# Down product of two token chunks by seven products of half-size blocks instead of eight, its block sums made on VectorE and GpSimd

## The chip, the cores and the metric

The kernel runs on one core of a Trainium2 chip. The metric is device time in microseconds (us) of one execution; the profile's span runs from the first to the last instruction of one such execution.

## What is computed

The reference is one step of a two-layer encoder trunk over 1024 prompt tokens and 64 sample tokens, all in float32. Only the last part of each layer matters here, the down-projection of the feed-forward part; the rest is projection, gating, attention and a recurrent memory.

```python
D_MODEL = 1024; DEPTH = 2; SEQ = 1024; DEC_SEQ = 64; D_FF = 2816; CONV_W = 3

def conv_ffn(x, g, w_up, conv_w, conv_b, w_down, conv_buf):
    up = rmsnorm(x, g) @ w_up
    T = up.shape[1]
    full = jnp.concatenate([conv_buf.astype(up.dtype), up], axis=1)
    c = conv_b + full[:, 0:T] * conv_w[0]
    for j in range(1, CONV_W):
        c = c + full[:, j:j + T] * conv_w[j]
    y = (jax.nn.gelu(c[..., :D_FF], approximate=False) * c[..., D_FF:]) @ w_down
    return y, full[:, -(CONV_W - 1):]

def layer(x, pos, lp, cache):
    ...
    x = x + mixed @ lp['w_out']
    y, conv_state = conv_ffn(x, lp['ffn_norm'], lp['w_up'], lp['conv_w'], lp['conv_b'], lp['w_down'], conv_buf)
    x = x + y
    ...
```

## The kernel before

The program is written engine by engine, each engine's instructions in an order fixed by hand, with counting semaphores between the engines. No scheduler moves anything. All activations stand transposed: features on the 128 partitions, tokens along the free axis. The residual stream `xT` stays in SBUF. Its tokens (1024 prompt, 2 of padding, 64 sample) form three chunks, `CH`: 0 and 1 of 384 columns, 2 of 322.

**Split products.** A float32 product is made of three matmuls in a reduced format (`split3`, L321 to L325). Each operand is split into a high part (ScalarE rounds a copy) and a low part (VectorE subtracts the high part from the original), and TensorE adds high by high, high by low and low by high.

**The up stage.** For each of 22 pairs `p` of up-projection columns, TensorE makes products into PSUM, VectorE combines them (`take`, L2333), ScalarE and VectorE do the convolution (`conv_first`, `tap`), the GELU and the gate product (`gate_product`, L2375), and SyncE stores the 128x1090 result to a DRAM scratch (`store_g`). `value_end` is the second half of that chain for the pair before. GpSimd makes sums of weight blocks here (`weight_sum`, L1978).

**The down stage.** The output has 8 blocks of 128 features, one PSUM bank each. For each chunk `c` and each of the 22 blocks `f` of 128 gate rows there is one step, `i = 22 c + f`:

- SyncE loads the weight row block `w_down[f]`, 128x1024 (`load_down`, 512 KB), and the gate block of the chunk, 128x384 (`load_g`, 192 KB);
- ScalarE makes the high parts (`down_high` L1716, `gate_high` L1722), VectorE the low parts (`down_low` L2380, `gate_low` L2385). The gate parts go round in four slots, so a high part of step `i` waits until TensorE is through with step `i - 4`;
- TensorE does 8 output blocks by 3 matmuls, 24 in a step (`step`), 1056 for chunks 0 and 1 of a layer.

When a chunk ends, VectorE adds the 8 banks into `xT` (`add_down`, L2062), ScalarE squares the result and GpSimd sums the squares for the next norm (`norm_add`, L371). In the last layer chunk 2 runs in two halves of 4 output blocks (`half_step`, with L2478 and L1824 for its weights).

**Names.** In the trace the gate blocks stand as `tHf` (as loaded), `tH` (high) and `tL` (low), the weights as `raw` and `wb`, and `sqE`, `sqn` and `acc` belong to the norm. DVE is VectorE, ACT ScalarE, POOL GpSimd, SP SyncE, PE TensorE.

## Time and profile before

| | before |
|---|---|
| time, median of 3 runs | 2478.15 us (2477.4 to 2478.68) |
| span of the profiled execution | 2478.2 us |
| PE (TensorE) busy | 2446.6 us, 99% of the span |
| DVE (VectorE) busy | 1588.2 us, 64% |
| ACT (ScalarE) busy | 1096.2 us, 44% |
| POOL (GpSimd) busy | 527.5 us, 21% |
| DMA | 265.89 MB, mean 107 GB/s |

The profiled execution took, by its span, what the timed runs took. Shares of busy time are means over stages with different limits: a 44% or 21% says nothing about a single stage. Matmuls are pipelined, so the durations in their rows overlap; the distance between two starts is what one costs.

### The profile page before, as it was taken

How to read it: one execution, taken by the hardware profiler on the slowest of the kernel's cores; microseconds unless marked ns; L12 is line 12 of the kernel's file. 1: busy time of each engine (PE TensorE's matmuls, PEld its weight loads, DVE VectorE, ACT ScalarE, POOL GpSimd, SP SyncE). 2: the span in 40 equal slices, each digit the busy share in tenths (PEclk: the TensorE clock that was granted, in tenths of full speed). 3: DMA queues.
4: the chain of work that ended last, by engine and by line, in shares of the span. 5: the costliest groups of instructions: out<-in, count | busy, mean ns of one | idle time of the engine just before them, and what ended most of it. 6: DMA issues, size and time to landing. Idle time of an engine off the chain costs nothing.

```text
span 2478.2 us, 41945 instructions
## 1 busy us (share of the span) xinstructions
PE 2446.6 (99%) x16611; PEld 2381.6 (96%) x16611; DVE 1588.2 (64%) x2693; ACT 1096.2 (44%) x2067; POOL 527.5 (21%) x490
## 2 busy tenths in 40 slices
PE   9999999999999999999999999999999999999999
PEld 8999888999999999999999988889999999999999
DVE  3115688878888887465611266878888888864564
ACT  6326656534333333343433355645334333343453
POOL 0001253423222220010110112433322222200110
PEclk9999999999999999999999999999999999999999
DMA  4442322122222223554525333212222222155564
GB/s 153 132 133 92 115 84 77 54 70 65 75 79 70 79 77 110 191 175 160 190 71 155 110 97 115 82 49 71 66 75 79 70 79 77 63 167 169 176 195 146
DMA packets 238072, 265.89 MB, mean 107 GB/s; under 512 B 15639, under 2 KB 207925, under 8 KB 235701
## 3 DMA queue, kind: packets, MB, share of 16 engines
q1 hardware_dynamic: 237876, 263.22, 33.5%
q8 instruction: 132, 2.16, 0.4%
q14 instruction: 64, 0.52, 0.1%
HBM read 213.06 MB, written 50.11 MB: 106 GB/s over the span
## 4 chain that ended last, share of the span: by engine, by line
PE 87%; DVE 6%; issue 3%; ACT 2%; DMA 1%; POOL 0%; SPq 0%; DVEq 0%; POOLq 0%; ACTq 0%
PE bank L323 27%; PE bank L325 26%; PE bank L324 26%; PE bank L1119 1%; PE bank L1046 1%; DMA zb<-z_scratch 1%; PE bank L1104 1%; PE bank L1088 1%; DVE actL L2265 1%; PE bank L1129 1%; PE bank L1068 1%; DVE hc L2201 0%; PE bank L1080 0%; DMA rawB<-in_w_down 0%; PE bank L999 0%
## 5 line engine op out<-in xcount | busy, mean ns | idle before, releaser
L323 PE MATMUL bank<-actH,wb 128*128 128x384 f32 (+1 forms) x1712 | 560.4, 327 | 1.8 <-DVE xT L2062 1.8
L324 PE MATMUL bank<-actL,wb 128*128 128x384 f32 (+1 forms) x1712 | 554.8, 324 | 0.0
L325 PE MATMUL bank<-actH,wb 128*128 128x384 f32 (+1 forms) x1712 | 554.4, 324 | 0.0
L323 PE MATMUL bank<-wzH,actH 128*128 128x256 f32 (+3 forms) x1296 | 369.1, 285 | 3.2 <-DVE wzL L2019 2.1
L325 PE MATMUL bank<-wzH,actL 128*128 128x256 f32 (+3 forms) x1296 | 364.2, 281 | 0.0
L324 PE MATMUL bank<-wzL,actH 128*128 128x256 f32 (+3 forms) x1296 | 363.8, 281 | 0.0
L323 PEld LDWEIGHTS bank<-actH,wb 128*128 128x128 f32 x1712 | 322.4, 188 | 7.2 <-issue 6.2
L324 PEld LDWEIGHTS bank<-actL,wb 128*128 128x128 f32 x1712 | 323.1, 189 | 0.7
L325 PEld LDWEIGHTS bank<-actH,wb 128*128 128x128 f32 x1712 | 323.2, 189 | 0.0
L323 PEld LDWEIGHTS bank<-wzH,actH 128*128 128x128 f32 (+1 forms) x1296 | 236.3, 182 | 6.1 <-issue 4.0
L323 PE MATMUL bank<-tH,wb 128*128 128x384 f32 x704 | 237.0, 337 | 1.2 <-ACT vn L1817 1.2
L324 PE MATMUL bank<-tL,wb 128*128 128x384 f32 x704 | 236.7, 336 | 0.0
L325 PE MATMUL bank<-tH,wb 128*128 128x384 f32 x704 | 236.7, 336 | 0.0
L324 PEld LDWEIGHTS bank<-wzL,actH 128*128 128x128 f32 (+1 forms) x1296 | 236.4, 182 | 0.0
L325 PEld LDWEIGHTS bank<-wzH,actL 128*128 128x128 f32 (+1 forms) x1296 | 236.1, 182 | 0.0
L1700 ACT ACTIVATE cv<-upb,convc 128x1090 f32<-128x1090 f32 x88 | 114.4, 1300 | 240.5 <-DVE upb L2357 240.3
L2380 DVE TENSOR_TENSOR wb<-raw,wb 128x1024 fp32r<-128x1024 f32 x88 | 107.8, 1225 | 169.7 <-ACT wb L1716 169.6
L1978 POOL TENSOR_TENSOR Sf<-raw 128x512 f32<-128x512 f32 x80 | 112.0, 1401 | 391.3 <-PE bank L325 382.5
L1674 ACT ACTIVATE Sx<-Sf 128x512 fp32r<-128x512 f32 x160 | 100.5, 628 | 200.1 <-POOL Sf L1978 200.1
L2333 DVE TENSOR_TENSOR upb<-bank,upb 128x384 f32<-128x384 f32 x280 | 148.1, 553 | 60.5 <-PE bank L325 57.5
L1444 ACT ACTIVATE zst<-bank,stat 128x256 f32<-128x256 f32 (+3 forms) x162 | 75.8, 473 | 240.9 <-PE bank L325 240.6
L1716 ACT ACTIVATE wb<-raw 128x1024 fp32r<-128x1024 f32 x88 | 93.2, 1061 | 198.7 <-PE bank L325 160.7
(311 smaller groups left out, 5152.5 us busy)
## 6 DMA issues: line engine op xcount, KB each, us to landing
raw<-in_w_up SPq DMA_DIRECT2D x88, 512.0 KB, 4.4
raw<-in_w_down SPq DMA_DIRECT2D x88, 512.0 KB, 3.6
g_scratch<-cv SPq DMA_DIRECT2D x44, 545.0 KB, 3.2
rawz<-in_w_in SPq DMA_DIRECT2D x22, 1024.0 KB, 5.4
zb<-z_scratch SPq DMA_DIRECT2D x16, 1156.0 KB, 5.4
tHf<-g_scratch SPq DMA_DIRECT2D x88, 192.0 KB, 3.7
z_scratch<-zst SPq DMA_DIRECT2D x128, 128.0 KB, 1.7
raw<-in_w_out SPq DMA_DIRECT2D x128, 128.0 KB, 2.8
```

The source lines that it names most:

```text
L323: pe.matmul(out, aH, bH, start=first, stop=False)
L324: pe.matmul(out, aH, bL, start=False, stop=False)
L325: return pe.matmul(out, aL, bH, start=False, stop=last)
L1046: m = pe.matmul(bank[2 * c + p // 2][64 * v:64 * v + 64, (p % 2) * 256 + k0:(p % 2) * 256 + k1], bqT[64 * v:64 * v + 64, p, 64 * c:64 * c ...
L1068: pe.matmul(bank[6][:, 0:4 * r], ones[0:r, :], dA[0:r, 0:4 * r], start=True, stop=True).then_inc(S["A_r"], 1)
L1444: act.activation(zst[0:r, u % 3, 0:w], bank[z_bank(u)][0:r, 0:w], ACT.Gelu if u < 18 else ACT.Copy, scale=rt[0:r, t:t + 1]).then_inc(z_ev, 1)
L1674: act.activation(Sx[:, s, 0], Sf[:, s, 1], ACT.Copy).then_inc(s_h, 1)
L1700: act.activation(cv[:, :], (upb2 if h else upb1)[:, PAD:], ACT.Identity, scale=convc[:, f + 88:f + 89], bias=convc[:, f + 132:f + 133]).th ...
L1716: act.activation(h, t, ACT.Copy).then_inc(w_h, 1)
L1978: pool.tensor_tensor(Sf[:, s, 1], x, y, ALU.add if s == 0 else ALU.subtract).then_inc(s_r, 1)
L2333: dve.tensor_tensor(out, bank[b][:, 0:out.shape[1]], other, ALU.mult if i in (6, 9) else ALU.add).then_inc(take_r, 1)
L2380: dve.tensor_tensor(lo, t, h.bitcast(F32), ALU.subtract).then_inc(w_l, 1)
```

## The change

The down product of chunks 0 and 1 together is a matrix of 1024 output features by 768 tokens, with 2816 rows to sum over. It is cut into halves three ways. Call the weight blocks A11 (features 0 to 511, gate rows 0 to 1407), A12 (features 0 to 511, gate rows 1408 to 2815), A21 and A22 (the same for features 512 to 1023), and the gate blocks B11, B12 (gate rows 0 to 1407, chunk 0 and 1), B21, B22 (gate rows 1408 to 2815). Eight block products become seven, each of 4 output blocks by 11 gate-row blocks (`NJ`) by 384 tokens, 12 matmuls in a step, 77 steps (`seven`), 924 matmuls:

| product q | weights | gates | added into |
|---|---|---|---|
| 0 | A21 + A22 (GpSimd) | B11 | C21, -C22 |
| 1 | A22 | B21 - B11 (GpSimd) | C11, C21 |
| 2 | A12 - A22 (GpSimd) | B21 + B22 (GpSimd) | C11 |
| 3 | A11 + A22 (GpSimd) | B11 + B22 (VectorE) | C11, C22 |
| 4 | A12 + A11 (GpSimd) | B22 | -C11, C12 |
| 5 | A11 | B12 - B22 (GpSimd) | C12, C22 |
| 6 | A21 - A11 (GpSimd) | B11 + B12 (VectorE) | C22 |

A weight tile is now 128x512 (256 KB, `load_tile`), kept in `at0` and `at1`; some are loaded again because the sums overwrite them. Gate blocks are loaded three rows at a time (`load_gates`) into `gT`, `actG` and `actF`. Chunk 2 keeps its steps, with other buffers and waits. The core of the diff:

```diff
@@ -497,30 +543,58 @@
+        def a_sum_at(l, i):
+
+            return l * N_SUM + 4 * (NF - 2) + (0, 0, 1, 2, 3, 0, 4)[i // NJ] * NJ + i % NJ + 1
+
+        def seven_bank(q, m):
+            return bank[m if q % 2 else 4 + (m + 2) % 4]
...
@@ -772,26 +846,60 @@
+                def load_tile(n, slot, f, h):
+
+                    tile_landed(sp, l, n - 7)
+                    n += NTOK + l * N_TILES
+                    sp.dma_start(a_tile(slot), w_down[f * P:f * P + P, 512 * h:512 * h + 512]).then_inc(tile_in[n % 7], 16)
...
@@ -813,16 +921,49 @@
                     if p == NF - 2:
-                        load_down(0)
-                        load_down(1)
-                for i in range(4):
-                    load_g(i)
-                load_down(2)
-                load_down(3)
+                        sp.wait_ge(w_l, weight_at(l, NF - 1, 1))
+                        sp.wait_ge(s_r, sum_at(l, NF - 1, 3))
+                        sp.wait_ge(mm, tile_mm(l, NF - 2, N_TILE))
+                        for j in range(3):
+                            load_first(j)
+                for j in range(3, 6):
+                    load_first(j)
+                sp.wait_ge(mm, tile_mm(l, NF - 1, 3))
+                for g in range(4):
+                    load_gates(0, g)
+                sp.wait_ge(mm, tile_mm(l, NF - 1, N_TILE))
+                for j in range(6, 9):
+                    load_first(j)
                 store_g(NF - 1)
+                for j in range(9, NJ):
+                    load_first(j)
...
@@ -1285,34 +1422,53 @@
+                def seven(i):
+
+                    q, j = i // NJ, i % NJ
+                    h, lo = (t.rearrange("p k n -> p (k n)") for t in seven_hl(i))
+                    pe.wait_ge(w_l, down_at(l, i))
+                    pe.wait_ge(b_l, gate_at(l, i))
+                    for m in range(4):
...
+                        s = slice(m * P, m * P + P)
+                        x = split3(pe, seven_bank(q, m)[:, 0:384], h[:, s], lo[:, s], gH[:, i % 4], gL[:, i % 4], j == 0, j == NJ - 1)
+                        if m == 3 or j == NJ - 1:
+                            x.then_inc(mm, 1)
...
@@ -1706,19 +1861,43 @@
+                def seven_high(i):
...
+                    act.wait_ge(mm, seven_mm(l, i - 4) if i >= 4 else tile_mm(l, NF - 1, (2, 4, 5, 7)[i]))
+                    act.activation(seven_hl(i)[0], a_tile(a_slot(q, j)).rearrange("p (k n) -> p k n", n=P), ACT.Copy).then_inc(w_h, 1)
+
+                def seven_gate_high(i):
...
+                    act.wait_ge(mm, seven_mm(l, i - 4) if i >= 4 else tile_mm(l, NF - 1, 2))
+                    act.activation(gH[:, i % 4], g_place(q // 4, j) if q in (0, 4) else gR[:, i % 4], ACT.Copy).then_inc(b_h, 1)
...
@@ -1997,8 +2201,44 @@
+                def a_sum(i):
...
+                    pool.tensor_tensor(t, x, y, ALU.subtract if q in (2, 6) else ALU.add).then_inc(s_r, 1)
+
+                def g_sum(i):
...
+                    pool.wait_ge(b_l, gate_at(l, i - 4))
+                    x, y = (gT[:, j], g_place(0 if q == 1 else 1, j))
+                    pool.tensor_tensor(gR[:, i % 4], x, y, ALU.add if q == 2 else ALU.subtract).then_inc(gs_r, 1)
+
                 n = 2 * l + 2
-                for c in range(3):
+                for i in range(N_SEVEN):
+                    if i // NJ in (0, 2, 3, 4, 6):
+                        a_sum(i)
+                    if i // NJ in (1, 2, 5):
+                        g_sum(i)
+                    m = i - 5 * NJ - 5
+                    if 1 <= m < KT:
+                        norm_add(pool, n, 0, m)
+                for c in range(1, 3):
...
@@ -2374,13 +2614,43 @@
+                def seven_gate_sum(i):
+
+                    q, j = i // NJ, i % NJ
+                    gates_landed(dve, l, (8 if q == 3 else 12) + j // 3)
+                    dve.wait_ge(b_l, gate_at(l, i - 4))
+                    dve.tensor_tensor(gR[:, i % 4], g_place(0, j), g_place(1, j) if q == 3 else gT[:, j], ALU.add).then_inc(gd_r, 1)
+
+                def seven_add(q):
+
+                    dve.wait_ge(bank_free, F0 + ADDED[q])
+                    for m in range(4):
+                        dve.wait_ge(mm, seven_mm(l, q * NJ + NJ - 1, m))
+                        for sign, r, c in OUTS[q]:
+                            x, y = xT[:, 4 * r + m, 384 * c:384 * c + 384], seven_bank(q, m)[:, 0:384]
+                            dve.tensor_tensor(x, x, y, ALU.add if sign > 0 else ALU.subtract).then_inc(bank_free, 1)
...
@@ -2505,38 +2774,33 @@
+                for i in range(4, N_SEVEN):
+                    if i + 2 < N_SEVEN and (i + 2) // NJ in (3, 6):
+                        seven_gate_sum(i + 2)
+                    seven_low(i)
+                    seven_gate_low(i)
+                    if i % NJ == 3 and i > NJ:
+                        seven_add(i // NJ - 1)
```

VectorE at the end of the up stage (the last pair of layer 0), before. `upb` and `cv` are the convolution's tiles:

```order
L2385 TENSOR_TENSOR tL<-tHf,tH 128x384 x4
L2333 TENSOR_TENSOR upb<-bank,rowS 128x322
...
L2380 TENSOR_TENSOR wb<-raw,wb 128x1024
L2367 SCALAR_TENSOR_TENSOR cv<-upb,convc,cv 128x1090
L2370 SCALAR_TENSOR_TENSOR cv<-upb,convc,cv 128x1090
L2375 TENSOR_TENSOR cv<-cv,cu 128x1090
L2380 TENSOR_TENSOR wb<-raw,wb 128x1024 x2
```

The same place of the changed kernel. L2621 is `seven_low`, L2628 `seven_gate_low`:

```order
L2628 TENSOR_TENSOR tL<-actG,tH 128x384 x2
L2573 TENSOR_TENSOR upb<-bank,rowS 128x322
...
L2607 SCALAR_TENSOR_TENSOR cv<-upb,convc,cv 128x1090
L2610 SCALAR_TENSOR_TENSOR cv<-upb,convc,cv 128x1090
L2615 TENSOR_TENSOR cv<-cv,cu 128x1090
L2628 TENSOR_TENSOR tL<-actG,tH 128x384
L2621 TENSOR_TENSOR wS<-at,wS 128x512
```

Before, the low gate parts of steps 0 to 3 stood ahead of the last convolution; now those of steps 2 and 3 stand behind it.

GpSimd between the up stage and the next norm (layer 0), before:

```order
L1978 TENSOR_TENSOR Sf<-Sf,raw 128x512
L1978 TENSOR_TENSOR Sf<-raw 128x512
L1978 TENSOR_TENSOR Sf<-raw,Sf 128x512
L371 TENSOR_TENSOR acc<-acc,sqE 128x384 x9
L400 TENSOR_TENSOR stat<-stat 128x3
```

The same place of the changed kernel, cut after the first two steps of product 2 and taken up again where product 3 begins. L2217 is `a_sum`, L2230 `g_sum`, L410 `norm_add`:

```order
L2182 TENSOR_TENSOR Sf<-raw,Sf 128x512
L2217 TENSOR_TENSOR at<-at 128x512 x11
L2230 TENSOR_TENSOR tHf<-gT,actG 128x384 x6
L2230 TENSOR_TENSOR tHf<-gT,actF 128x384 x5
L2217 TENSOR_TENSOR at<-at 128x512
L2230 TENSOR_TENSOR tHf<-gT,actG 128x384
L2217 TENSOR_TENSOR at<-at 128x512
...
L2217 TENSOR_TENSOR at<-at 128x512 x22
L2230 TENSOR_TENSOR tHf<-gT,actG 128x384 x6
L2230 TENSOR_TENSOR tHf<-gT,actF 128x384
L410 TENSOR_TENSOR acc<-acc,sqn 128x384
```

Where GpSimd had only the norm's sums there are now 55 weight sums and 33 gate sums in a layer, in the order of the steps.

## Rows read from the trace of the kernel before

**Rows 1.** The page: the span.

```profile
span 2478.2 us, 41945 instructions
```

**Rows 2.** Windows: A:B length, busy of PE, PEld, DVE, ACT, POOL; PEclk, DMA share, GB/s.

```profile
370.00:400.00 30.00, 29.50 (x216) 26.29 (x215) 24.62 (x62) 17.11 (x53) 11.30 (x14) 1.00 0.19 63
973.00:1158.50 185.50, 184.90 (x1060) 184.53 (x1059) 96.78 (x119) 75.41 (x107) 8.59 (x7) 1.00 0.55 179
2194.00:2379.00 185.00, 184.40 (x1057) 184.03 (x1056) 91.27 (x111) 74.65 (x109) 8.58 (x7) 1.00 0.55 179
```

**Rows 3.** Timeline of PE: start, duration; steps 0 and 44 begin the first and last.

```profile
973.00 0.34 PE L323 MATMUL bank<-tH,wb 128*128 128x384 f32 x1
...
1119.38 0.33 PE L324 MATMUL bank<-tL,wb 128*128 128x384 f32 x1
...
1129.51 0.34 PE L325 MATMUL bank<-tH,wb 128*128 128x384 f32 x1
...
1158.51 0.31 PE L323 MATMUL bank<-tH,wS 128*128 128x322 f32 x1
```

**Rows 4.** Groups by line and shape: count, busy us, mean ns, idle before.

```profile
L1978 POOL TENSOR_TENSOR Sf<-raw,Sf 128x512 f32<-128x512 f32 x40 | 52.4, 1310 | 164.6 <-PE bank L325 164.6
L2385 DVE TENSOR_TENSOR tL<-tHf,tH 128x384 fp32r<-128x384 f32 x88 | 59.9, 683 | 1.4 <-ACT tH L1722 1.4
L2062 DVE TENSOR_TENSOR xT<-bank,xT 128x384 f32<-128x384 f32 x64 | 33.5, 553 | 16.0 <-PE bank L325 15.9
L1824 ACT ACTIVATE wb<-raw 128x512 fp32r<-128x512 f32 x44 | 26.5, 624 | 14.0 <-DMA raw<-in_w_down 8.6 <-PE bank L325 5.0
```

**Rows 5.** Timelines of DVE and of POOL near 915 us (up stage).

```profile
915.43 1.22 DVE L2254 TENSOR_TENSOR wb<-raw,wb 128x1024 fp32r<-128x1024 f32 x1
916.57 2.67 DVE L2333 TENSOR_TENSOR upb<-bank,upb 128x384 f32<-128x384 f32 x5
...
915.77 2.03 POOL L1978 TENSOR_TENSOR Sf<-Sf,raw 128x512 f32<-128x512 f32 x1 [2.75 <-PE bank L325]
```

**Rows 6.** Timelines of DVE and of POOL near 2390 us (last chunk).

```profile
2389.07 1.20 DVE L2478 TENSOR_TENSOR wb<-raw,wb 128x512 fp32r<-128x512 f32 x1 [0.18 <-ACT wb L1824]
2390.20 1.31 DVE L2483 TENSOR_TENSOR actL<-tHf,actH 128x322 fp32r<-128x322 f32 x1
2391.43 0.55 DVE L2062 TENSOR_TENSOR xT<-bank,xT 128x384 f32<-128x384 f32 x1
...
2388.71 1.02 POOL L371 TENSOR_TENSOR acc<-acc,sqE 128x384 f32<-128x384 f32 x1
2389.89 1.27 POOL L371 TENSOR_TENSOR acc<-acc,sqE 128x384 f32<-128x384 f32 x1 [0.17 <-ACT sqE L362]
```

**Rows 7.** Timeline of DVE, two low parts in a row with POOL idle.

```profile
2397.27 0.68 DVE L2478 TENSOR_TENSOR wb<-raw,wb 128x512 fp32r<-128x512 f32 x1
2397.87 0.48 DVE L2483 TENSOR_TENSOR actL<-tHf,actH 128x322 fp32r<-128x322 f32 x1
2398.28 0.68 DVE L2478 TENSOR_TENSOR wb<-raw,wb 128x512 fp32r<-128x512 f32 x1
```

**Rows 8.** Timelines of DVE, ACT and SPq where the up stage of layer 0 ends.

```profile
973.27 0.49 DVE L2333 TENSOR_TENSOR upb<-bank,rowS 128x322 f32<-128x322 f32 x1 [0.20 <-PE bank L325]
979.17 1.30 DVE L2375 TENSOR_TENSOR cv<-cv,cu 128x1090 f32<-128x1090 f32 x1
...
963.07 0.53 ACT L1722 ACTIVATE tH<-tHf 128x384 fp32r<-128x384 f32 x1 [6.34 <-DMA tHf<-g_scratch]
974.12 1.04 ACT L1716 ACTIVATE wb<-raw 128x1024 fp32r<-128x1024 f32 x1
...
959.68 1.78 SPq L794 DMA_DIRECT2D tHf<-g_scratch  x4
```

**Rows 9.** DMA issues of the page and of 940 to 990 us: count, KB each, us to landing.

```profile
raw<-in_w_down SPq DMA_DIRECT2D x44, 256.0 KB, 3.1
...
GB/s 0 0 0 0 0 0 138 393 308 0 13 0 0 0 0 202 281 194 243 381 344 256 13 0 0 0 0 0 0 0 0 13 0 391 154 295 291 390 79 115
```

More of the change, by code:

```diff
@@ new lines, in _ @@
+                for j in range(NJ):
+                    load_a11(j)
+                for g in range(4):
+                    sp.wait_ge(gs_r, g_sum_at(l, 2 * NJ + min(3 * g + 3, NJ) - 1))
+                    load_gates(3, g)
+                for j in range(NJ):
+                    load_a12_again(j)
+                for j in range(9):
+                    load_a21_again(j)
+                def load_half(j):
+                    h, f = j // NF, j % NF
+                    if j < 4:
+                        sp.wait_ge(mm, tile_mm(l, NF - 1, N_TILE))
+                    else:
+                        sp.wait_ge(w_l, down_at(l, LAST0 + j - 4))
@@ L1804, in _ @@
                     else:
-                        for i in range(4):
-                            gate_high(i)
+                        seven_gate_high(0)
+                        seven_gate_high(1)
                     conv_first(p, 0)
@@ new lines, in square_second @@
+                def square_second(m):
+                    norm_square(act, n, 1, m, F0 + (ADDED[5] + 2 * m + 1 if m < 4 else ADDED[6] + m - 3))
+                if l + 1 == DEPTH:
+                    for j in range(2 * NF):
+                        half_high(j)
+                        if j < NF:
+                            gate_high_last(j)
+                        m = j - 3
+                        if 0 <= m < KT:
+                            square_second(m)
+                            act.activation(xT[:, m, 384:768], xT[:, m, 384:768], ACT.Copy,
```

539 lines of the change are left out of this document (328 added, 211 removed).

## The prediction, made before the changed kernel ran

> **What bounds the kernel now.** I read the page first: the span is 2478.2 us [rows 1]. The windows of the two stretches in which chunks 0 and 1 of a layer run say what sets the pace there: PE is busy 184.90 of 185.50 us at a granted clock of 1.00, DVE 96.78, ACT 75.41, POOL 8.59 [rows 2]. So TensorE is the bound, the others keep ahead of it, and GpSimd is nearly unused. The timeline of PE gives the price of a matmul by its starts: 59 of them from 1119.38 to 1129.51, 58 distances, 0.1747 us each; and the 1056 matmuls of chunks 0 and 1 take from 973.00 to 1158.51, 185.5 us [rows 3]. Layer 1 has the same stretch.
>
> **What TensorE gains.** 77 steps of 12 matmuls are 924 in place of 1056. At 0.1747 us that is 161.4 us, 24.1 less per layer, 48 us in the two. A step is now 12 x 0.1747 = 2.10 us, half of before, and in each step ScalarE and VectorE must still deliver one weight part and one gate part. Were TensorE still the bound, the time would be 2430 us. ScalarE is no danger: 0.62 for a 128x512 copy [rows 4] and, by the first gate copy, 0.53 [rows 8], 1.2 of 2.10 us.
>
> **What the sums cost.** The trace shows that an operation of GpSimd and one of VectorE that reads two SBUF tensors do not run at the same time. Near 2390 us [rows 6]: GpSimd works to 2389.73 (2388.71 + 1.02); VectorE's low part of a weight, issued at 2389.07, ends at 2390.27, 0.54 after it; GpSimd's next, issued at 2389.89, ends at 2391.16, 0.89 after VectorE's; VectorE's next low part ends at 2391.51, 0.35 after that. They take turns, even when VectorE's second one was already queued. Near 915 us [rows 5] it is GpSimd that waits: VectorE ends at 916.65, GpSimd at 917.80, 1.15 after, for a 128x512 sum that takes 1.31 undisturbed [rows 4]. VectorE's operations with one operand in PSUM are not in this: five ran in 2.67 us under that sum [rows 5], and one at 2391.43 in 0.55 [rows 6]. The Trainium skill says the same (SBUF — State Buffer, section Who interferes with whom): the second to issue blocks fully, if VectorE has two SBUF inputs; by that rule, the trace agrees, with 0.54, 0.89 and 0.35 us behind the other's end.
>
> So there is a shared resource, call it the port, and I add up how long it is held in one layer's chunks 0 and 1. GpSimd: 55 weight sums of 128x512 at 1.15, 63.3 us; 33 gate sums of 128x384 at 0.89, 29.4; 7 norm sums at 0.89, 6.2 (they are moved in here from chunk 1, where the port was free). VectorE: 77 low parts of 128x512 at 0.54 and 77 of 128x384 at 0.42 (0.35 x 384/322), 73.9; 22 gate sums at 0.42, 9.2. Together 182 us, in a stretch where TensorE needs 161.4. The 48 additions from PSUM (before 16) cost VectorE 12 x 4 x 0.48 = 23 us, but no port. The port, not VectorE (about 120 us) or GpSimd (about 110), is what becomes scarce.
>
> How a step goes then: with a low part pair (0.96) and nothing else 0.96; each GpSimd operation that lies between adds its hold. Product 1 (one gate sum): 1.85 us in a step, under 2.10. Product 2 (weight and gate sum): 0.96 + 1.15 + 0.89 = 3.0. Product 3 and 6 (weight sum, VectorE's gate sum): 2.53. Products 0 and 4: 2.11. The lead that may cover the excess is short: a high part of step i waits for TensorE's step i - 4, so VectorE is 3 steps ahead at most, and a gate sum of GpSimd waits for the low part of step i - 4, so GpSimd is 4 steps ahead of VectorE.
>
> **The walk through one layer**, TensorE's delay product by product:
>
> - Start of product 0. VectorE's take of the last pair starts when TensorE is through (973.27), then comes the last convolution, whose gate product ended at 980.47 [rows 8]. In the new order the low gate part of step 2 stands behind that. A 1.04 us high part [rows 8] ahead of that convolution becomes 0.62 [rows 4], so step 2 can begin at about 980.1 + 0.5 = 980.6, where TensorE wants it at 973.0 + 2 x 2.10 = 977.2: 3.4 us. Further, the first gate blocks (issued at 959.68 before, used at 963.07 [rows 8]) now queue behind the store of 545 KB and six tiles of 256 KB, 2.1 MB, which at the 250 to 390 GB/s of the bursts [rows 9] are 6 to 8 us; they arrive near 967.5, and VectorE has two low gate parts and the last pair's takes behind them. Three weight sums of GpSimd fall in the same stretch. That moves the chain by 2 to 3 us more. I take 6 us, between 3.4 and 9.
> - Products 0 and 1 are then paced by TensorE. From VectorE's step 18 GpSimd is already at product 2, so its last four steps go at 3.0: 1.2 us late.
> - Product 2. VectorE delivers step 25 about 9 us after the product begins, then adds product 1 (8 additions, 3.8 us), during which GpSimd comes to its 4-step limit. Steps 26 to 28 take 3.0 each. Then GpSimd, through with the product, runs ahead into the 11 weight sums of product 3, which wait for nothing of VectorE's; turn by turn each of VectorE's operations meets one: steps 29 and 30 cost 0.96 + 2 x 1.15 = 3.26, steps 31 and 32, with the gate sums for 33 and 34, 1.38 + 3 x 1.15 = 4.8. Sum from the start: 9 + 3.8 + 1 + 6 + 6.5 + 9.6 = 36, and the last step's own 2.1: 38 us in place of 23.1, 15.0 late.
> - Product 3 finds its sums made: 0. Product 4: the additions of product 3 use up the lead, 1.2.
> - Products 5 and 6. From step 61 to 65 gate and norm sums come in turns (2.7 a step), then GpSimd runs ahead into 11 weight sums and two norm sums while VectorE does 62 to 66 at 3.3 to 4.8 each; then product 5's additions. Product 5 takes 30.3, product 6 28.3, together 12.5 late.
>
> Sum of the delays: 6 + 1.2 + 15.0 + 0 + 1.2 + 12.5 = 36 us. A layer's stretch: 161.4 + 36 = 197.4 against 185.5, +11.9; two layers +23.8. 2478.2 + 23.8 = 2502 us; the timed median is the span's to 0.1. Moving the tail changes nothing: chunk 2 steps are long (24 matmuls) or as before. DMA traffic falls (66 tiles of 256 KB for 44 loads of 512), and 179 GB/s at a share of 0.55 [rows 2] left room; a 256 KB load lands in 3.1 us [rows 9], so the tiles, asked for some 9 steps ahead, are hidden; uncovered they would cost 3 us each. The clock: a 30 us window with DMA waits kept 1.00 [rows 2], so I count no loss.
>
> **Bounds.** If turns packed without any idle port time, the stretch is 182 less what is done before TensorE arrives (6 weight sums and the first low parts, 9 us), 173, perhaps 178 with the start: 2478 - 2 x 7.5 = 2463 us. If each operation costs its undisturbed distance (GpSimd 1.31 [rows 4] and 1.02 [rows 6], VectorE 0.60 between starts [rows 7] and 0.47), the port sum is 206, 24 more per layer, some 12 of it in the crowded products, and the start 9 instead of 6: 2502 + 2 x 13 = 2528. I take the turn-taking prices, since those rows are the same operations under the same pressure. Another price: the Trainium skill (GPSIMD Engine Reference, section Instruction dispatch) gives a two-input GpSimd body a floor of about 2.5 cycles per element. An estimate from that page, at its 1.2 GHz, is 1.07 us for 128x512 and 0.80 for 128x384; by it the sum for the port would be 174 instead of 182 and the time about 2490. The rows show 1.15 and 0.89.
>
> **Rivals.**
> - *TensorE stays the bound* (6 in 100): the short rings absorb the turns and only the start is late. For it: VectorE was busy half of the stretch and GpSimd hardly [rows 2]. Against: 182 us held in 161. It gives 2478 - 2 x (24.1 - 6) = 2442, faster.
> - *The port packs well* (18 in 100): products 2, 5 and 6 are crowded, but 0, 1 and 4 take the overflow, as GpSimd works ahead. This is the rival on the other side. It decides where the delays of a layer fall under 24.1 us instead of 36, that is, where each of the 95 GpSimd operations holds VectorE up 0.13 us less than counted. Against: VectorE's 4-slot limit forbids work ahead. It gives 2455 to 2485, centre 2468; 11 of the 18 faster, 4 within 0.2%, 3 slower.
> - *The start and the queue are worse* (10 in 100): the gate blocks land several us later, or the port's undisturbed prices hold; 2520 to 2540.
> - The forecast, the port as the bound with short leads, has 66 in 100: 2485 to 2520, 2502 the likeliest.
>
> **Numbers.** No change that can be told is within 0.2%, 5 us. Faster 0.17 (6 + 11), same 0.05 (4 and the low edge of the forecast), slower 0.78. The range runs from 2460, which leaves out the first rival and the lowest part of the second, to 2528, which leaves out most of the third: about 2 in 10 outside.
>
> **What would show it.** 924 matmuls in each layer's stretch, still 0.175 us apart when fed, clock 1.00; idle PE ahead of the high-by-high matmul put down to VectorE's low parts, some 30 us a layer, most of it in the third, sixth and seventh product; VectorE's low parts of 128x512 with a mean near 1.2 us instead of the 0.68 of [rows 7], and in the first and fifth product near 0.7; GpSimd's weight sums taking 1.7 to 1.9; step 2 of the first product beginning 3 to 9 us late. I am wrong if low parts stay at 0.7 and 0.55 us beside a busy GpSimd, if the waits are for DMA or for ScalarE, or if the delays of a layer are under 24 us.

## The result and the profile after

The changed kernel takes 2532.5 us (2529.8 to 2539.5, 4 runs), the one before 2477.8 us (2476.5 to 2478.7, 4 runs, same chip): a ratio of 1.0226, 95% interval 1.0211 to 1.0241, 55 us slower. The forecast was slower, 2502 us, with a range to 2528: the sign is right, the time lies 4.5 us above the range and 30 above the forecast. The profiled execution is the slowest of the four, 5 us above their median, so the profile's sums are a little larger than the timed difference. From here on products are counted first to seventh, as they run; the first is q = 0 of the table (the recorded expectations use both counts: "gate sums of products 1, 2 and 5" goes by q, "product 5 from 29.8" is the fifth).

The page of the changed kernel answers to [rows 1]:

```profile
span 2537.7 us, 42355 instructions
...
PE 2440.6 (96%) x16347; PEld 2360.6 (93%) x16347; DVE 1783.3 (70%) x2933; ACT 1129.0 (44%) x2199; POOL 783.8 (31%) x666
...
PE   9999999999999998898999999999999999988798
...
DVE  3115687888888887989611267877888888789874
...
POOL 0001244432222223864000113442322222358610
```

In the 16th to 19th and the 36th to 39th slice (of 63.4 us), where chunks 0 and 1 are, VectorE stands at 8 and 9, GpSimd at up to 8, and TensorE has holes. The windows of the stretch in layer 0, cut where the seven products begin (by the starts of every 132nd matmul), answer to [rows 2]; behind the length stand busy time of PE, PEld, DVE, ACT and POOL, then the granted clock:

```profile
971.40:1008.50 37.10, 29.37 (x137) 28.20 (x136) 28.98 (x38) 15.67 (x27) 12.05 (x11) 0.82 0.78 270
1008.50:1033.30 24.80, 23.72 (x134) 23.05 (x132) 24.46 (x29) 11.85 (x23) 17.91 (x14) 1.00 0.07 26
1033.30:1071.20 37.90, 28.68 (x132) 26.46 (x133) 37.90 (x36) 11.49 (x22) 33.56 (x23) 0.86 0.26 82
1071.20:1095.20 24.00, 23.59 (x134) 23.30 (x133) 23.72 (x33) 11.75 (x22) 16.66 (x8) 1.00 0.61 212
1095.20:1125.00 29.80, 25.54 (x133) 24.57 (x133) 23.57 (x34) 11.50 (x22) 15.28 (x12) 0.94 0.38 124
1125.00:1157.50 32.50, 27.30 (x134) 25.07 (x132) 31.81 (x31) 16.01 (x31) 27.44 (x20) 0.89 0.02 3
1157.50:1186.70 29.20, 25.36 (x132) 24.82 (x133) 27.07 (x43) 11.44 (x20) 5.61 (x4) 0.94 0.22 69
```

A product of 132 matmuls at 0.1747 us takes 23.06 us; the stretch is 215.3 us instead of 185.5. In layer 1 it is 214.9. The account closes: 2478.2 + 29.8 + 29.4, less 3.4 us by which the two up stages end earlier, plus 3.7 us in the tail, is 2537.7. In the third and the sixth product VectorE is busy 37.90 of 37.90 and 31.81 of 32.50 us: it is the engine that does not get through. What keeps it so long is in the groups by line and shape, which answer to [rows 4] (mean ns of one stands behind the busy time):

```profile
L2217 POOL TENSOR_TENSOR at<-at 128x512 f32<-128x512 f32 x110 | 184.1, 1691 | 91.3 <-DMA at<-in_w_down 91.0
L2621 DVE TENSOR_TENSOR wS<-at,wS 128x512 fp32r<-128x512 f32 x154 | 167.6, 1091 | 30.4 <-ACT wS L1874 30.4
L2628 DVE TENSOR_TENSOR tL<-tHf,tH 128x384 fp32r<-128x384 f32 x110 | 105.3, 957 | 0.0
L2645 DVE TENSOR_TENSOR xT<-xT,bank 128x384 f32<-128x384 f32 x96 | 46.0, 542 | 2.7 <-PE bank L361 2.7
```

Undisturbed, the low parts (L2621 and L2628) are 0.68 and 0.55 us; the additions from PSUM (L2645) kept their 0.54. The timelines of DVE and of POOL late in the fourth product and early in the fifth show single ones:

```profile
1097.09 1.78 DVE L2621 TENSOR_TENSOR wS<-at,wS 128x512 fp32r<-128x512 f32 x1
1098.79 1.64 DVE L2628 TENSOR_TENSOR tL<-actG,tH 128x384 fp32r<-128x384 f32 x1
```

```profile
1081.54 23.30 POOL L2217 TENSOR_TENSOR at<-at 128x512 f32<-128x512 f32 x11 [5.80 <-DMA at<-in_w_down]
```

GpSimd has eleven weight sums in a row here, and from the second on each of VectorE's operations with two SBUF inputs is 1.1 us longer than its own time, one hold of a sum. The first of the eleven is another case (timelines of POOL and of DVE):

```profile
1081.54 6.99 POOL L2217 TENSOR_TENSOR at<-at 128x512 f32<-128x512 f32 x1 [5.80 <-DMA at<-in_w_down]
...
1087.66 1.42 DVE L2621 TENSOR_TENSOR wS<-at,wS 128x512 fp32r<-128x512 f32 x1 [0.28 <-ACT wS L1874]
```

It is held out for 5.7 us, while eleven of VectorE's operations with two SBUF inputs pass back to back at their own 0.54 to 0.68 us, and gets through at VectorE's first pause, of 0.28 us; from then on the two alternate. Sums of 6.5 to 8.5 us stand in layer 1 as well and in three of the runs below (fillers, order of the start, gate sums on VectorE). So a turn is not given at once; here the two engines alternate only after a pause of VectorE.

The adds from PSUM are not in this. In the third product eight of them take 3.79 us, and two of GpSimd's sums run under them in 0.86 and 1.28:

```profile
1041.91 3.79 DVE L2645 TENSOR_TENSOR xT<-xT,bank 128x384 f32<-128x384 f32 x8
...
1043.11 0.86 POOL L2230 TENSOR_TENSOR tHf<-gT,actF 128x384 f32<-128x384 f32 x1
1043.92 1.28 POOL L2217 TENSOR_TENSOR at<-at 128x512 f32<-128x512 f32 x1
```

The first product starts late for a wait that stands ahead of it. In the timelines of ACT and of DVE, ScalarE waits 8.88 us for the first gate block, and VectorE, whose order is fixed, 7.11 us for the high part of it, with the last pair's takes and convolution behind:

```profile
969.77 0.94 ACT L1886 ACTIVATE tH<-actG 128x384 fp32r<-128x384 f32 x2 [8.88 <-DMA actG<-g_scratch]
970.33 1.03 DVE L2628 TENSOR_TENSOR tL<-actG,tH 128x384 fp32r<-128x384 f32 x2 [7.11 <-ACT tH L1886]
```

The waits of TensorE over the whole kernel (total, times, longest):

```profile
PE bank L359 <- DVE tL L2628: 53.0, 39, 3.3
PE bank L359 <- DVE upb L2573: 12.8, 6, 3.7
```

What the prediction put at nothing is in the timeline of PE after such a wait: matmuls of 384 columns begin 0.32 us apart, at half the pace.

```profile
978.86 0.52 PE L360 MATMUL bank<-tL,wS 128*128 128x384 f32 x1
979.18 0.52 PE L361 MATMUL bank<-tH,wS 128*128 128x384 f32 x1
979.50 0.52 PE L359 MATMUL bank<-tH,wS 128*128 128x384 f32 x1
```

Such distances (0.25 to 0.62 us) occur 117 times in layer 0 and 109 times in layer 1, and hold 16.5 and 14.7 us more than 0.1747 each; the true gaps hold 35.8 and 37.1. The sum, 31 us over both layers, is just what the forecast is short of, which looks like the whole explanation. The third experiment shows that it is not.

### The profile page after: what moved, and what is told of

Read it like the earlier page. It is cut to its first block, busy times and chain, and to the rows that moved or that the text cites. A ratio compares the mean times of both kernels' runs of the same rounds, so it can differ in the third digit from the quotient of the medians.

```text
span 2537.7 us, 42355 instructions
## 1 busy us (share of the span) xinstructions
PE 2440.6 (96%) x16347; PEld 2360.6 (93%) x16347; DVE 1783.3 (70%) x2933; ACT 1129.0 (44%) x2199; POOL 783.8 (31%) x666
## 4 chain that ended last, share of the span: by engine, by line
PE 77%; DVE 15%; issue 2%; DMA 2%; ACT 2%; SPq 0%; POOL 0%; DVEq 0%; ACTq 0%; POOLq 0%
PE bank L359 23%; PE bank L361 23%; PE bank L360 23%; DVE wS L2621 4%; DVE tL L2628 4%; DVE xT L2645 2%; PE bank L1184 1%; PE bank L1256 1%; PE bank L1225 1%; DVE cv L2610 1%; PE bank L1241 1%; DMA actG<-g_scratch 1%; PE bank L1266 1%; PE bank L1205 1%; DVE actL L2505 0%
## 5 line engine op out<-in xcount | busy, mean ns | idle before, releaser
L359 PE MATMUL bank<-actH,wb 128*128 128x384 f32 (+1 forms) x1680 | 551.4, 328 | 1.8 <-DVE xT L2302 1.8
L360 PE MATMUL bank<-actL,wb 128*128 128x384 f32 (+1 forms) x1680 | 545.7, 325 | 0.0
L361 PE MATMUL bank<-actH,wb 128*128 128x384 f32 (+1 forms) x1680 | 545.2, 324 | 0.0
L359 PEld LDWEIGHTS bank<-actH,wb 128*128 128x128 f32 x1680 | 317.1, 189 | 7.3 <-issue 6.2
L359 PE MATMUL bank<-tH,wS 128*128 128x384 f32 (+1 forms) x728 | 259.7, 357 | 65.2 <-DVE tL L2628 53.0
L360 PEld LDWEIGHTS bank<-actL,wb 128*128 128x128 f32 x1680 | 317.7, 189 | 0.7
L361 PEld LDWEIGHTS bank<-actH,wb 128*128 128x128 f32 x1680 | 317.7, 189 | 0.0
L360 PE MATMUL bank<-tL,wS 128*128 128x384 f32 (+1 forms) x728 | 254.6, 350 | 0.0
L361 PE MATMUL bank<-tH,wS 128*128 128x384 f32 (+1 forms) x728 | 254.0, 349 | 0.0
L359 PEld LDWEIGHTS bank<-tH,wS 128*128 128x128 f32 x728 | 145.4, 200 | 81.1 <-issue 54.2
L2217 POOL TENSOR_TENSOR at<-at 128x512 f32<-128x512 f32 x110 | 184.1, 1691 | 91.3 <-DMA at<-in_w_down 91.0
L2621 DVE TENSOR_TENSOR wS<-at,wS 128x512 fp32r<-128x512 f32 x154 | 167.6, 1091 | 30.4 <-ACT wS L1874 30.4
```

The source lines that it names most:

```text
L359: pe.matmul(out, aH, bH, start=first, stop=False)
L360: pe.matmul(out, aH, bL, start=False, stop=False)
L361: return pe.matmul(out, aL, bH, start=False, stop=last)
L2217: pool.tensor_tensor(t, x, y, ALU.subtract if q in (2, 6) else ALU.add).then_inc(s_r, 1)
L2621: dve.tensor_tensor(lo, a_tile(a_slot(i // NJ, i % NJ)).rearrange("p (k n) -> p k n", n=P), h.bitcast(F32), ALU.subtract).then_inc(w_l, 1)
```

## The experiments

**Theory A**: a sum of GpSimd and a two-input operation of VectorE take turns; VectorE, kept waiting, is late; TensorE waits for it. The rivals below say what else it could be.

**No sums.** GpSimd's 88 sums of a layer shrink to one column; the gate parts of the second, third and sixth product read unsummed gates.

```
-  pool.tensor_tensor(t, x, y, ...).then_inc(s_r, 1)
+  pool.tensor_tensor(t[:, 0:1], x[:, 0:1], y[:, 0:1], ...).then_inc(s_r, 1)
-  pool.tensor_tensor(gR[:, i % 4], x, y, ...).then_inc(gs_r, 1)
+  pool.tensor_tensor(gR[:, i % 4, 0:1], x[:, 0:1], y[:, 0:1], ...).then_inc(gs_r, 1)
```

> The changed kernel with every sum of GpSimd in the stretch of chunks 0 and 1 (55 weight sums, 33 gate sums) cut to one column, signals kept, and the gate parts of products 1, 2 and 5 made from the unsummed gates, so those sums are left out of the result. Theory A (the two-input sums of GpSimd and the low parts of VectorE take turns on a way to SBUF, TensorE comes late for it, and then runs its matmuls at 0.32 us): low parts of weights fall from a mean of 1.09 to about 0.68 us and of gates to 0.55 everywhere, third product from 38 to about 23.5 us, seventh from 29 to 23.5, only the start and the gate sums of VectorE in products 3 and 6 still cost something; a layer's stretch 215 to about 172 us, kernel 2445 us (2435 to 2460). Rival B (the loss is landing transfers and the order of the steps, not the sums): products stay within 3 us of what they are, 2515 or more.

Measured 2453.4 us, ratio to the kernel before 0.9909 (0.9895 to 0.9924). The window of layer 0, then the groups of the low parts:

```profile
974.67:1146.70 172.03, 167.28 (x928) 166.29 (x927) 132.42 (x232) 87.34 (x166) 34.78 (x89) 0.98 0.42 140
```

```profile
L2621 DVE TENSOR_TENSOR wS<-at,wS 128x512 fp32r<-128x512 f32 x154 | 110.3, 718 | 70.2 <-ACT wS L1874 70.2
...
L2628 DVE TENSOR_TENSOR tL<-tHf,tH 128x384 fp32r<-128x384 f32 x44 | 24.1, 548 | 0.0
```

As theory A had it: 79 us of time hang on GpSimd's sums. From the second product on, each takes 23.3 us. VectorE is busy 132.4 us in place of 197.5, so 88 sums cost it 65 us, 0.74 each. The first product still takes 32.1 us: a delay of 9 us over 23.06 is there without the sums. VectorE still waits 5.1 us there for the first high part of a gate block.

**Memsets in place of sums.** GpSimd writes the sum's tile and reads nothing: first 8 or 6 memsets of 64 columns, then, since those took it only 0.70 us a sum, 20 or 16 short ones.

```
-  pool.tensor_tensor(t, x, y, ...).then_inc(s_r, 1)
+  for u in range(20):
+      x = pool.memset(t[:, 512 * u // 20:512 * (u + 1) // 20], 1.0)
+  x.then_inc(s_r, 1)
```

> Each sum of GpSimd in the stretch is replaced by 8 (weights) or 6 (gates) memsets of 64 columns into the sum's own tile, about 1.2 and 0.9 us of GpSimd's time by the memset rows (0.204 us for 128 columns, 0.526 for 512), so it works as long as before but reads nothing; the sums are left out of the result. Theory A1 (what the sum holds is the way by which two inputs are read): low parts at 0.68 and 0.55 us, time as in the run without sums, 2450 us (2440 to 2470). Rival A2 (any GpSimd operation holds it, writes too): low parts stay near 1.1 and 0.95, 2520 to 2535. Rival C (GpSimd is simply too slow a link in the chain, sum then high part then low part, whoever shares what): low parts 0.68 but the third product stays over 30 us and the kernel over 2490, with TensorE's waits ending in ACT or POOL rather than at the end of a long low part.

> As the run with memsets, since its 8 and 6 memsets took GpSimd only about 0.70 and 0.52 us in place of 1.15 and 0.89: here 20 and 16 shorter ones, about 1.15 and 0.9 us by a fixed part of 0.036 us each and 0.43 us for 512 columns, read from the distance of 0.087 us between memsets of 64. The sums are left out of the result. Theory A1 (only operations with two SBUF inputs take turns with VectorE's): 2454 us within 8, low parts at 0.55 to 0.72. Rival C (GpSimd's own time in the chain sum, high part, low part is what cost in the changed kernel): over 2475, TensorE waiting for low parts that began late and were not long.

Measured 2454.4 us, ratio 0.9907 (0.9890 to 0.9924), and for the longer ones 2454.1 us, 0.9909 (0.9894 to 0.9924). Of the longer ones, a window in the third product (POOL is the fifth busy time) and the groups:

```profile
1028.00:1052.00 24.00, 24.00 (x138) 24.00 (x137) 19.71 (x38) 11.88 (x23) 19.90 (x363) 1.00 0.47 146
```

```profile
L2625 DVE TENSOR_TENSOR wS<-at,wS 128x512 fp32r<-128x512 f32 x154 | 114.1, 743 | 69.7 <-ACT wS L1874 69.7
...
L2632 DVE TENSOR_TENSOR tL<-tHf,tH 128x384 fp32r<-128x384 f32 x110 | 64.2, 583 | 0.0
```

GpSimd is busy 19.9 of 24 us, and TensorE never waits. So GpSimd's time in the chain (rival C) costs nothing that can be told, and neither do its writes in pieces of 24 to 64 columns (rival A2); what costs is what the sums do beyond that, their reads. The low parts are 0.03 us longer than without sums. As the pieces begin 0.05 to 0.09 us apart, a hold as short as one piece could hide in that: a write as long as a sum was not run. The Trainium skill (SBUF — State Buffer, section Who interferes with whom) says it so: VectorE with two SBUF inputs contends with a GpSimd instruction that reads SBUF, not with one that only writes. These runs agree as far as short writes go, 2454 us with the writes and 2453 with almost nothing.

**Filler matmuls.** Zeros times the identity, added into a sum that is open, ahead of 19 waits.

```
+  for k in range(FILL.get(i, 0)):          # 1 to 11, by the gap there
+      pe.matmul(seven_bank(q, 0)[0:96, 0:128], nul[:, :], ident[:, :], start=False, stop=False)
   pe.wait_ge(w_l, down_at(l, i))
```

> The changed kernel with filler matmuls (zeros times the identity, 128 columns, f32, added into an open sum, so they change nothing) ahead of the waits of 19 steps of each layer, as many as fill the gap that the trace of the changed kernel shows there (1 to 11 of 0.27 us). Theory A, clock lost on the path: matmuls at 0.32 us vanish (226 in the changed kernel, 31 us over both layers) and most of that comes back: 2508 us (2500 to 2518). Rival D (the slow matmuls only fill time in which TensorE would have waited for VectorE anyway): matmuls at 0.175 but the gaps grow by as much, 2528 to 2536.

Measured 2526.6 us, ratio 1.0202 (1.0187 to 1.0217): 6 us less, nearly rival D. The windows of the third, fourth and sixth product:

```profile
1028.90:1065.30 36.40, 32.69 (x199) 30.75 (x200) 36.40 (x34) 11.48 (x22) 33.03 (x23) 1.00 0.26 80
1065.30:1094.10 28.80, 24.48 (x134) 22.85 (x132) 28.80 (x35) 11.99 (x22) 16.63 (x12) 1.00 0.54 182
1121.70:1153.90 32.20, 27.65 (x161) 26.28 (x160) 31.32 (x30) 15.89 (x31) 27.22 (x20) 1.00 0.01 4
```

The clock is 1.00, and VectorE is full or nearly so in them: the third product is 1.5 us shorter than it was, the fourth 4.8 longer, the sixth as before. The half-speed distances hold about 12 us in both layers in place of 31; the gaps hold 85 in place of 73. Of 19 us of restored pace TensorE gave back 12 in longer gaps, 6 reached the end. So most of the 31 us was not what the forecast lacked, close as the two numbers are. The run doesn't tell whether fillers that outlast a wait cost part of the 6 to 19 us themselves.

**The order of the start.**

```
   seven_gate_low(1)
+  seven_gate_low(2)
   take(p, 6, ...)
...
+  seven_low(3); seven_gate_low(3)          # were behind the last value tile
   tap(p, 1, 1)
```

On ScalarE the high parts of gates 2 and 3 move ahead of the last convolution, on SP two gate groups ahead of weight tiles 3 to 5.

> Order of the start alone: gate low part 2 ahead of take 6, weight and gate low part 3 ahead of the last two taps of the last value tile, the high parts of gates 2 and 3 ahead of the last convolution's first part on ScalarE, and the first two groups of gates asked for ahead of weight tiles 3 to 5. Theory A (step 2 and 3 of the first product wait for VectorE's value chain, then run at half clock): first product 37 to about 30 us in each layer, 2519 us (2512 to 2527). Rival E (something else in the last value tile is late by as much once these are early, take 9 or the gate product, on which bank 7 and the rows for chunk 2 wait): first product stays over 35 us, 2528 to 2540.

Measured 2523.7 us, ratio 1.0193 (1.0178 to 1.0208): 9 us less. The window of the first product, then the timeline of DVE in it:

```profile
971.87:999.90 28.03, 24.05 (x137) 23.42 (x136) 24.48 (x30) 13.34 (x24) 14.30 (x10) 1.00 0.73 250
```

```profile
976.90 2.27 DVE L2608 SCALAR_TENSOR_TENSOR cv<-upb,convc,cv 128x1090 f32<-128x1090 f32 x1
979.21 2.27 DVE L2611 SCALAR_TENSOR_TENSOR cv<-upb,convc,cv 128x1090 f32<-128x1090 f32 x1
981.51 2.25 DVE L2616 TENSOR_TENSOR cv<-cv,cu 128x1090 f32<-128x1090 f32 x1
```

The first product fell from 37.1 to 28.0 us, as expected; only half of those 9 us a layer reached the end (by the two profiles 12.7 of 18). The products behind it took part back (the second went from 24.8 to 26.3, the seventh from 29.2 to 30.5). The edit changes two things at once, the order on VectorE and ScalarE and the order of the loads: the first gate block is now used at 964.10 instead of 969.77, and VectorE waits 1.1 us for it instead of 7.1. Which of the two gives how much was not run. The last value tile's operations now meet GpSimd's weight sums, 2.27 us in place of 1.35.

**All gate sums on VectorE.** GpSimd keeps the 55 weight sums.

```
-  if i // NJ in (1, 2, 5):
-      g_sum(i)                             # GpSimd
...
-  if i + 2 < N_SEVEN and (i + 2) // NJ in (3, 6):
+  if i + 2 < N_SEVEN and (i + 2) // NJ in (1, 2, 3, 5, 6):
       seven_gate_sum(i + 2)                # VectorE
```

> The changed kernel with the gate sums of products 1, 2 and 5 on VectorE as well (all 55 there, GpSimd keeps the 55 weight sums). Theory A (sums and low parts take turns, GpSimd's gate sum holds 0.89 us of it, VectorE's about 0.42): the turns of a layer fall from 182 to about 160 us, the third product from 38 to about 29 us, the sixth from 32 to about 25, the fourth rises or stays, no change of the start; 2495 us (2480 to 2512). Rival F (VectorE's own time is the bound, since it takes 33 more operations of 0.55 us a layer): the third product stays over 34 us and the kernel is not under 2525.

Measured 2521.0 us, ratio 1.0180 (1.0163 to 1.0197), a miss: 12 us less, not 37. The third product did fall, to 23.4 us, but the second rose to 29.3 and the fourth to 32.1, VectorE full in it:

```profile
1060.20:1092.30 32.10, 25.90 (x133) 24.40 (x131) 32.10 (x34) 12.44 (x23) 22.50 (x15) 0.95 0.47 154
```

The expectation's 160 us of turns is a slip: by its own prices 182 falls by 33 x (0.89 - 0.42) to 166.5, a little over the 161 that TensorE needs. But the stretch is 205.3 us, 39 more than that. The count was of the wrong resource: what runs out is VectorE's time, its own 148 us of work plus what GpSimd's sums add to it, 189.5 together. That also gives the small gain: a gate sum of GpSimd had cost VectorE (197.5 - 189.5) / 33 + 0.47 = 0.71 us, its own costs 0.47, so only 8 us a layer of VectorE's time came free.

**The last gate block later on the queue**, alone and with the two edits before.

```
   for j in range(NJ):
+      if 5 <= j < 9:                       # was a loop ahead of this one
+          sp.wait_ge(gs_r, g_sum_at(l, 2 * NJ + min(3 * (j - 5) + 3, NJ) - 1))
+          load_gates(3, j - 5)
       load_a12_again(j)
```

> The changed kernel with the four loads of the last block of gates moved behind the fifth to eighth load of the fifth product's weight tiles, on the same queue, nothing else. Theory A (the weight tiles of the fifth product waited in SP's queue behind those gates, which wait for the third product's gate sums, so ten weight sums of GpSimd came in one block): product 5 from 29.8 to about 25 us, 2521 us (2514 to 2528). Rival G (the sums are late for the turns they take, wherever the tiles are): product 5 stays at 28 to 30 us or the loss shows in the next, 2529 to 2538.

> The order of the start of the run before together with all gate sums on VectorE. Theory A: both gains add, since they lie in different products: 9 us of the start and what the gate sums on VectorE give by themselves, 2486 us (2472 to 2504). Rival F (VectorE is full once the queue at the start is gone): the sum of the two gains falls short by more than 8 us.

> As the run before, with the last block of gates asked for behind the fifth to eighth weight tile of the fifth product too. Theory A: a few us less again, 2478 us (2464 to 2500), so about where the kernel before is; what then stays is the start (first product some 28 us against 23) and the waits behind the adds of VectorE. Rival G: no different from the run before within 2 us.

Alone: 2535.2 us, 1.0233 (1.0218 to 1.0248), no gain. GpSimd's sums of the fifth product, of which eleven stood in one block, came one by one (timeline of POOL), and the fourth and the fifth product became (windows):

```profile
1073.41 1.44 POOL L2217 TENSOR_TENSOR at<-at 128x512 f32<-128x512 f32 x1 [1.19 <-DMA at<-in_w_down]
1075.94 1.55 POOL L2217 TENSOR_TENSOR at<-at 128x512 f32<-128x512 f32 x1 [1.09 <-DMA at<-in_w_down]
```

```profile
1069.22:1096.90 27.68, 25.00 (x134) 22.84 (x134) 27.68 (x36) 12.20 (x22) 14.35 (x11) 1.00 0.56 189
1096.90:1123.20 26.30, 23.83 (x134) 23.16 (x134) 24.98 (x33) 11.52 (x22) 11.94 (x10) 1.00 0.45 145
```

54.0 us for the two against 53.8: rival G. Each sum takes its time from VectorE whenever it comes, and the loss only moved into the product before: there VectorE, which makes gate sums of its own in it, is now busy 27.68 of 27.68 us. The start and the gate sums together: 2507.8 us, 1.0126 (1.0111 to 1.0141), 25 us less than the changed kernel where the single gains, 9 and 12, make 21: they add. My 2486 carried the miss of the gate sums along. With the later gate block too: 2514.7 us, 1.0151 (1.0136 to 1.0166), 7 us worse; which wait makes it worse I did not follow.

**The adds in four parts.** One part behind each of the next product's fourth to seventh low parts.

```
-  if i % NJ == 3 and i > NJ:
-      seven_add(i // NJ - 1)
+  if 3 <= i % NJ < 7 and i > NJ:
+      seven_add(i // NJ - 1, i % NJ - 3)   # the two or one adds of one bank
```

> The changed kernel with VectorE's adds of a product cut into four parts, one behind each of the next product's fourth to seventh low parts, instead of all behind the fourth; nothing else. Theory K (VectorE is the bound from the third product on, busy 197 us of a stretch of 215, of which about 0.73 us for each of GpSimd's 88 sums; the adds are as long in four parts): the waits of 2.6 us at the fourth step of products 3 to 7 break into shorter ones, and the time falls little, 2525 us (2517 to 2533). Rival L (the block of adds is itself what takes the lead away, 2.6 us and a half-speed step in five products of each layer): 2512 us or less.

Measured 2521.7 us, ratio 1.0186 (1.0170 to 1.0201): 11 us less, inside the range of theory K, though more than its 7; rival L, at 2512 or less, fails. The block of adds costs some of the lead, but most of the loss stays.

**Weight sums on VectorE too**, all but the eleven of the first product; then with the order of the start; then with the adds in four parts.

```
+  if i + 2 in ON_DVE:                      # third, fourth, fifth, seventh product
+      dve.tensor_tensor(t, x, y, ...).then_inc(sd_r, 1)
```

> The run with all gate sums on VectorE, and the weight sums of products 3, 4, 5 and 7 on VectorE too (44 of 55; GpSimd keeps the eleven of the first product). Theory K (a sum of GpSimd costs VectorE 0.74 us of waiting, a weight sum of its own 0.61 to 0.68): VectorE's busy time in a stretch falls from 189 to about 183 us though it does 44 more operations, low parts are 0.68 and 0.55 us from the third product on, 2509 us (2499 to 2519). Rival M (VectorE's own work counts in full and the waiting was mostly slack): 2530 or more, since it gets 27 us a layer more to do.

> The run before with the changed order of the start. Theory K: beside the run with the start's order and the gate sums on VectorE (2508 us) it falls by the same 12 us as the run before beside its own, 2496 us (2486 to 2506). Rival M: 2515 or more.

> The run before with the adds in four parts as well. Theory K: with VectorE still the bound a few us less than the run before, 2491 us (2478 to 2504), so still not under the kernel before. Rival L: under 2482.

Measured 2483.4 us, ratio 1.0028 (1.0017 to 1.0039); 2470.0 us, 0.9971 (0.9959 to 0.9984); 2465.6 us, 0.9960 (0.9945 to 0.9975). Theory K had the sign and far too small a size, 12 us for the first where 38 were measured. The adds in four parts gave 4.4 us; that the last run lies under rival L's 2482 says nothing for rival L, since the run without the parts is at 2470 already. The window of layer 0 and the groups of the first, then the window of the third:

```profile
971.30:1157.30 186.00, 172.02 (x927) 166.91 (x926) 175.15 (x314) 88.67 (x166) 16.92 (x12) 0.96 0.39 131
```

```profile
L2607 DVE TENSOR_TENSOR wS<-at,wS 128x512 fp32r<-128x512 f32 x154 | 111.1, 723 | 13.7 <-ACT wS L1879 13.7
...
L2617 DVE TENSOR_TENSOR at<-at 128x512 f32<-128x512 f32 x88 | 60.2, 684 | 0.0
```

```profile
974.90:1152.10 177.20, 166.71 (x928) 161.84 (x927) 170.04 (x308) 85.90 (x163) 23.17 (x13) 1.00 0.40 134
```

VectorE does 44 operations more than in the run with the gate sums and is busy 14.3 us less, 175.2 against 189.5. Its own weight sums add 44 x 0.60 (0.68 long, 0.60 between starts) = 26.4, so the 44 of GpSimd had cost it 26.4 + 14.3 = 40.7 us, 0.93 each. The 0.74 that I had used was a mean over all 88: the 33 gate sums cost 0.71 each, and the eleven of the first product, where VectorE waits anyway, next to nothing. The count now closes: 132.4 (no sums) + 33 x 0.47 + 26.4 = 174.3, measured 175.2.

**Thirteen weight sums back on GpSimd, each held until VectorE adds from PSUM.**

```
+  if i in UNDER:
+      pool.wait_ge(bank_free, l * FREES + ADDED[UNDER[i]] + 1)
```

> The run with all sums on VectorE and the changed start, but 13 of its 44 weight sums back on GpSimd, each held until VectorE has begun the adds of the product named for it (three under each block of eight adds, one under the four of product 3). Theory K (a GpSimd sum costs VectorE nothing while VectorE adds from PSUM, and saves it 0.61 us of its own): low parts stay at 0.68 and 0.55, VectorE's busy time in a stretch falls by 8 us, 2460 us (2452 to 2468) against 2470 of the run it is made from. Rival N (the sums come late for their high part, or spill over the end of the adds and cost 1.1 us each there): 2470 or more.

Measured 2462.9 us, ratio 0.9940 (0.9924 to 0.9957), 7 us less than the run that it is made from, as theory K had it. Its window in layer 0, and from the timelines of POOL and of DVE one of its groups of three:

```profile
972.34:1150.20 177.86, 169.03 (x928) 165.24 (x927) 170.22 (x295) 86.78 (x163) 33.10 (x26) 0.98 0.41 138
```

```profile
1028.39 3.81 POOL L2223 TENSOR_TENSOR at<-at 128x512 f32<-128x512 f32 x3 [18.77 <-DVE xT L2647]
...
1027.70 3.80 DVE L2647 TENSOR_TENSOR xT<-xT,bank 128x384 f32<-128x384 f32 x8
1031.41 1.21 DVE L2638 TENSOR_TENSOR tHf<-gT,actF 128x384 f32<-128x384 f32 x1
```

Three sums in 3.81 us, their undisturbed length, and eight adds in 3.80. But the sums begin 0.7 us after the adds and end 0.7 after them: VectorE's next operation takes 1.21 in place of 0.55, as rival N had it in kind. The four groups of three take 1.9, 0.7, 0.65 and 0.6 us from VectorE in this way, 3.8 together. VectorE's busy time fell from 174.2 to 170.2, 4 us for the 7.8 expected (13 x 0.60), short by about that; the time fell as much as expected, 3.5 us a layer. The same thirteen sums without the wait were not run, so what the wait itself is worth is not shown. This version beats the kernel before by 13 us, and the changed one by 70.

## Why the prediction was right, and why it fell short

- *What TensorE gains*: right. 924 matmuls, 0.1747 us apart when fed; with nothing in the way from the second product on (the run without sums), 23.3 us a product.
- *Turns between GpSimd and VectorE*: right in kind and in price for the crowded places, though not a rule: a sum that comes while VectorE leaves no pause gets no turn (6.99 us for one of 1.27). Low parts of 1.64 and 1.78 us in the crowded places against 0.55 and 0.68 (means 1.09 where near 1.2 was forecast), weight sums of 1.69 (1.7 to 1.9), adds from PSUM untouched, and 79 us of the kernel's time gone with the sums. The Trainium skill (SBUF — State Buffer, section Who interferes with whom) makes VectorE's two SBUF inputs the condition. The trace agrees: under GpSimd's sums the adds from PSUM keep their 0.54 us (0.47 between starts).
- *The walk*, delays in us over 23.06 per product of layer 0, forecast and measured: first 6 and 14.0; second 1.2 and 1.7; third 15.0 and 14.9; fourth 0 and 0.9; fifth 1.2 and 6.8; sixth and seventh 12.5 and 15.6. Together 36 and 53.9. In the third product the walk is right step by step: its four steps at 3.26, 3.26, 4.8 and 4.8 took 3.00, 3.25, 4.80 and 4.78 on VectorE (its text has three steps at 3.0 before them, 9 us, its sum 7, the trace 5.8). **Two terms failed.** The *start of product 0* was taken at 6, between 3.4 and 9, and was 14.0: the low part of step 2 stood behind VectorE's value chain and began at 985.64, where the term had 980.1 and 2 to 3 us for the queue (timeline of DVE),

```profile
984.42 1.30 DVE L2615 TENSOR_TENSOR cv<-cv,cu 128x1090 f32<-128x1090 f32 x1
985.64 0.55 DVE L2628 TENSOR_TENSOR tL<-actG,tH 128x384 fp32r<-128x384 f32 x1
```

  while TensorE was ready at 971.4, not at 973.0. The term had the right causes at too small a price: the first gate block was used at 969.77 where it had 967.5, and VectorE stood still for it, so that everything behind came late. In the run without sums the delay is 9.0 still, so about 5 of the 14 go with the sums and 9 with the queue and the chain; the new order of low parts and loads took 9 of the 14 away, though the end kept only half of that (two thirds by the profiles). And *product 4, "the additions of product 3 use up the lead, 1.2"* (the fifth) was 6.8: the walk priced its steps at 2.11 us, one weight sum to a step, but the eleven sums came in a block, in which a step costs 3.26, the price that the walk itself gives for such a place. That the queue of the loads makes the block, and the block the loss, was my reading of the trace, and the run with the loads moved refuted it: the sums come one by one there, and the 54 us of the two products stay. Most of them run during the fourth product then, beside VectorE's own gate sums, where the walk had "0" for sums already made. So the eleven sums and the additions do not fit beside VectorE's work of these two products in either order that was run; how the 6.8 us divide between them stays open.
- *"The port ... is what becomes scarce", not VectorE (about 120 us)*: this is where the reasoning, not only a size, was wrong. A wait in turn is time of VectorE. With it VectorE is busy 197.5 of 215.3 us. Bringing the port count down to 166 us (the run with the gate sums) left 205.3; what helped most was to take GpSimd's weight sums away from beside VectorE's two-input operations, 38 us. The bound by perfect packing (2463 us) rests on that sum. The forecast rests on the walk, whose steps have the wait in them, which fits with the third product coming out right.
- *The clock, "I count no loss"*: wrong in what the trace shows, small in what it costs. The granted clock fell to 0.82 in the first product and 0.86 in the third; keeping it up gave 6 us of the 55. The 30 us window that the prediction went by could not show it: TensorE is busy 29.5 of 30.0 us there, with one gap of 0.5 us, where the changed kernel has gaps of 1.5 to 3.5.
- *DMA tiles hidden*: held for the weight tiles. TensorE waits for no load, and GpSimd's waits for tiles (91 us) cost nothing that the runs could find. It did not hold for the first gate block, see the start.
- *"Moving the tail changes nothing"*: 3.7 us too long in the tail, not followed up.
- *Bounds*: the upper one has 13 us a layer where its own terms, 12 and 3, make 15, so 2532 and not 2528. That this meets the measured time is luck: it goes by undisturbed prices for every operation, and the prices measured were those of the turns.
- *Rivals*: "the start and the queue are worse" (2520 to 2540, 10 in 100) is what came, and the start was the largest single miss, 8 of 18 us a layer; the fifth product is 5.6 of them, the sixth and seventh 3.1.

## What to carry to other kernels

An idle GpSimd is no free helper for sums of SBUF tensors beside a VectorE that does the same: here a 128x512 sum cost VectorE 0.93 us in its crowded products, and VectorE does it in 0.60. Hand GpSimd work for the time in which VectorE reads PSUM, begin it early enough to end there, and count a wait in turn as busy time of the engine that waits. Where a loss seen in the trace seems to explain what a forecast lacks (a lower clock, a block of sums behind late loads), take it away and time the kernel before it is believed: here two such losses were worth 6 us and nothing.
